# Norm boundaries of a diffusion trunk taken in two token blocks, latents then context

## The reference, cut to what matters

```python
def modulate(x, g, shift, scale):
    return rms_norm(x, g) * (1 + scale) + shift

def macaron_layer(x, mod, norm_g, ffn_in, ffn_out, mixer):
    m = mod[:, :, None, :]
    x = x + 0.5 * m[:, 2] * swiglu(modulate(x, norm_g[0], m[:, 0], m[:, 1]), ffn_in[0], ffn_out[0])
    mixed, own_kv = mixer(modulate(x, norm_g[1], m[:, 3], m[:, 4]))
    x = x + m[:, 5] * mixed
    x = x + 0.5 * m[:, 8] * swiglu(modulate(x, norm_g[2], m[:, 6], m[:, 7]), ffn_in[1], ffn_out[1])
    return x, own_kv
```

## Time and profile before

| | |
|---|---|
| Median of 3 runs | 1470.13 us (1469.03 to 1473.22) |
| The profiled execution | 1469.22 us, its span 1467.4 us |
| TensorE busy | 97% of the span |
| VectorE, ScalarE, GpSimd busy | 66%, 38%, 8% |
| Mean granted TensorE clock | 0.977 of full speed |
| DMA | 243 MB, mean 166 GB/s |

### The profile page before, as it was taken

How to read it: one execution, slowest core, us unless ns; L and a number is a source line. 1 busy time by engine, 2 the same in 40 slices (tenths; PEclk the granted TensorE clock), 3 DMA queues, 4 the chain that set the end, 5 groups by cost and what they waited for, 6 DMA issues and landing times.

```text
span 1467.4 us, 21457 instructions
## 1 busy us (share of the span) xinstructions
PE 1418.3 (97%) x8275; PEld 1388.5 (95%) x8275; DVE 973.9 (66%) x1417; ACT 554.9 (38%) x725; POOL 113.4 (8%) x105
## 2 busy tenths in 40 slices
PE   7999999999858999999999999999999999999999
PEld 5999999999737899999999999999999999999999
DVE  5788879668997668878526788888353459443322
ACT  3433332246575543333224433322345343333320
POOL 0000000016454100000001000000020010000000
PEclk9999999999878999999999999999999999999999
DMA  9765667424100256655341765674333135333432
GB/s 375 280 226 203 236 232 254 162 87 137 52 29 30 101 201 224 234 207 208 115 143 72 262 233 206 220 250 166 137 122 115 62 137 204 125 133 116 142 114 72
DMA packets 46086, 243.02 MB, mean 166 GB/s; under 512 B 5584, under 2 KB 8272, under 8 KB 25424
## 3 DMA queue, kind: packets, MB, share of 16 engines
q1 hardware_dynamic: 45744, 242.16, 45.7%
q10 hardware_dynamic: 288, 0.13, 0.0%
HBM read 240.57 MB, written 1.70 MB: 165 GB/s over the span
## 4 chain that ended last, share of the span: by engine, by line
PE 87%; DVE 9%; ACT 2%; issue 1%; DMA 0%; POOL 0%; SPq 0%; DVEq 0%; ACTq 0%; POOLq 0%
PE ps L1194 28%; PE ps L1196 27%; PE ps L1195 27%; DVE conv L981 4%; PE ps L1283 1%; DVE w_lo L771 1%; PE ps L1257 1%; DVE smax L1046 1%; PE ps L1264 1%; ACT w_hi L516 1%; PE ps L1570 0%; DVE prob L1056 0%; DVE e_sig L1056 0%; DMA x<-in_x_cols 0%; DVE n_full L847 0%
## 5 line engine op out<-in xcount | busy, mean ns | idle before, releaser
L1194 PE MATMUL ps<-a_hi,w_hi 128*128 128x384 f32 x1744 | 587.6, 337 | 4.3 <-DVE a_lo L1061 1.6
L1195 PE MATMUL ps<-a_lo,w_hi 128*128 128x384 f32 x1744 | 583.6, 335 | 0.0
L1196 PE MATMUL ps<-a_hi,w_lo 128*128 128x384 f32 x1744 | 583.5, 335 | 0.0
L771 DVE TENSOR_TENSOR w_lo<-w_raw,w_hi 128x2048 fp32r<-128x2048 f32 x153 | 353.1, 2308 | 213.9 <-ACT w_hi L516 213.9
L516 ACT ACTIVATE w_hi<-w_raw 128x2048 fp32r<-128x2048 f32 x153 | 292.0, 1909 | 239.0 <-DMA w_raw<-in_w_units 239.0
L1194 PEld LDWEIGHTS ps<-a_hi,w_hi 128*128 128x128 f32 x1744 | 328.3, 188 | 12.1 <-issue 3.3
L1195 PEld LDWEIGHTS ps<-a_lo,w_hi 128*128 128x128 f32 x1744 | 328.2, 188 | 0.1
L1196 PEld LDWEIGHTS ps<-a_hi,w_lo 128*128 128x128 f32 x1744 | 328.0, 188 | 0.0
L793 DVE SCALAR_TENSOR_TENSOR m_raw<-m_raw 128x1024 f32<-128x1024 f32 x256 | 299.2, 1220 | 0.0
L1196 PE MATMUL ps<-h_hi,w_lo 128*128 (+1 forms) x704 | 236.6, 336 | 0.0
L1195 PE MATMUL ps<-h_lo,w_hi 128*128 (+1 forms) x704 | 236.5, 336 | 0.0
(11 more groups left out here) (172 smaller groups left out, 710.0 us busy)
## 6 DMA issues: line engine op xcount, KB each, us to landing
w_raw<-in_w_units SPq DMA_DIRECT2D x153, 1024.0 KB, 4.9
m_raw<-in_w_rows SPq DMA_DIRECT2D x128, 512.0 KB, 5.7
m_raw<-in_w_pairs SPq DMA_DIRECT2D x5, 1024.0 KB, 15.6
p_raw<-in_w_pairs SPq DMA_DIRECT2D x3, 1024.0 KB, 24.7
x<-in_x_cols SPq DMA_DIRECT2D x2, 768.0 KB, 5.3
out<-x SPq DMA_DIRECT2D x8, 192.0 KB, 1.9
fourier<-in_k_fourier SPq DMA_DIRECT2D x1, 768.0 KB, 4.5
m_raw<-in_c_ctx SPq DMA_DIRECT2D x1, 512.0 KB, 5.4
```

The costliest lines, as they stand in the source:

```text
L771: nc.vector.tensor_tensor(w_lo[:, slot(u), :], w_raw[:, slot(u), :], w_hi[:, slot(u), :].bitcast(FP32), ALU.subtract).then_inc(lo_done, 1)
L1194: mm(out, whi, mhi, start=start, stop=False)
L1195: mm(out, whi, mlo, start=False, stop=False)
L1196: return mm(out, wlo, mhi, start=False, stop=stop)
```

## The change

The tokens are taken in two blocks, first the 256 latents, then the 128 context tokens (`BLOCKS`). At each of the five boundaries:

- The last two units close together. `closing` runs the 8 output tiles in the order 6, 7, 0 to 5 for the latents (12 matmuls each), then again for the context. The last FFN (s = 5) keeps its old width and only joins its last two units.
- `block_sums` and `block_spread` of the latents stand in TensorE's stream after the third and the fifth context tile of the closing; those of the context stand after the second and the sixth latent tile of the opening. Banks 6 and 7 hold them.
- `first_units` opens two units side by side for the latents, then for the context; at boundary 1 too. Every tile of weights is so loaded twice, once per block.
- Residual, square, scaled, high and low are one operation per tile and block, in an order written out in `turn` (VectorE) and `opening` (ScalarE). GpSimd adds seven squares per block. The splits of the next units stand among them.
- The idle products at boundaries 1 to 5 are gone.
- A load of SP that waits for the second-last unit now waits for both.

```diff
+BLOCKS = [(1, CTX, TOK), (0, 0, CTX)]
+BLOCK_TILES = [range(CTX // P, TT), range(0, CTX // P)]
+D_ORDER = [6, 7, 0, 1, 2, 3, 4, 5]
+ADDED = KT - 1
...
+        def closed(s, blk, i):
+            return 2 * KT * s + KT * blk + i + 1
+        def opened(n, blk, d):
+            return KT + 2 * KT * (n - 1) + KT * blk + d + 1
+        def block_step(n, blk):
+            return 2 * n + blk
...
-                for d in range(1, ADDED):
-                    pool.wait_ge(sq_done, KT * n + d + 1)
-                    if n > 1 or d > 1:
-                        pool.wait_ge(acc_done, (ADDED - 1) * (n - 1) + d - 1)
-                    first = n_sq[:, 0, :] if d == 1 else n_acc[:]
-                    nc.gpsimd.tensor_tensor(n_acc[:], first, n_sq[:, d, :], ALU.add).then_inc(acc_done, 1)
+                for blk, (_, lo, hi) in enumerate(BLOCKS):
+                    for i in range(1, ADDED):
+                        done = (ADDED - 1) * (2 * (n - 1) + blk) + i - 1
+                        pool.wait_ge(sq_done, opened(n, blk, i))
+                        if done:
+                            pool.wait_ge(acc_done, done)
+                        first = n_sq[:, D_ORDER[0], lo:hi] if i == 1 else n_acc[:, lo:hi]
+                        nc.gpsimd.tensor_tensor(n_acc[:, lo:hi], first, n_sq[:, D_ORDER[i], lo:hi], ALU.add).then_inc(acc_done, 1)
...
+            def square(n, blk, i):
+                _, lo, hi = BLOCKS[blk]
+                d = D_ORDER[i]
+                act.wait_ge(x_ready, opened(n, blk, i))
+                nc.scalar.activation(n_sq[:, d, lo:hi], x[:, d, lo:hi], ACT.Square).then_inc(sq_done, 1)
+            def root(n, blk):
+                t = BLOCK_TILES[blk]
+                act.wait_ge(ms_done, block_step(n, blk))
+                nc.scalar.activation(stat[:, 4 + t.start:4 + t.stop], stat[:, t.start:t.stop], ACT.Sqrt).then_inc(root_done, 1)
+            def high(n, blk, d):
+                cnd, lo, hi = BLOCKS[blk]
+                act.wait_ge(full_done, KT + opened(n, blk, d))
+                nc.scalar.activation(a_hi[:, d, lo:hi], n_full[:, d, lo:hi], ACT.Identity,
+                                     bias=m_shift[:, n, d, cnd:cnd + 1]).then_inc(a_hi_done, 1)
+            def opening(n):
+                preload(n, ACT.Sqrt)
+                for i in range(KT):
+                    square(n, 0, i)
+                    if i == 3:
+                        split(UNIT0[n] + 1)
+                square(n, 1, 0)
+                square(n, 1, 1)
+                root(n, 0)
+                square(n, 1, 2)
+                square(n, 1, 3)
+                for d in range(KT):
+                    high(n, 0, d)
+                    if d < 4:
+                        square(n, 1, 4 + d)
+                    if d == 5:
+                        root(n, 1)
+                split(UNIT0[n] + 2)
+                for d in range(KT):
+                    high(n, 1, d)
...
             split(u + 11)
-            split(u + 12)
             act.wait_ge(cache_out, 32)
-            norm_stats(2)
-            norm(2)
+            opening(2)
             ffn(2)
...
+            def residual(s, blk, i):
+                cnd, lo, hi = BLOCKS[blk]
+                d = D_ORDER[i]
+                if blk == 0 or i < KT - 1:
+                    dve.wait_ge(y_done, (2 * KT - 1) * s + KT * blk + i + 1)
+                else:
+                    dve.wait_ge(unit_done, RING + UNIT0[s + 1])
+                nc.vector.scalar_tensor_tensor(x[:, d, lo:hi], ps[:, d, lo:hi], m_gate[:, s, d, cnd:cnd + 1],
+                                               x[:, d, lo:hi], ALU.mult, ALU.add).then_inc(x_ready, 1)
...
+            def mean(n, blk):
+                t = BLOCK_TILES[blk]
+                dve.wait_ge(stat_done, block_step(n, blk))
+                nc.vector.tensor_scalar(stat[:, t.start:t.stop], ps[:, 7, t.start:t.stop], 1.0 / D_MODEL, RMS_EPS,
+                                        ALU.mult, ALU.add).then_inc(ms_done, 1)
+            def diagonal(n, blk):
+                t = BLOCK_TILES[blk]
+                a, b = 8 + t.start, 8 + t.stop
+                dve.wait_ge(root_done, block_step(n, blk))
+                dve.wait_ge(dve_self, mark(nc.vector.reciprocal(stat[:, a:b], stat[:, a - 4:b - 4])))
+                nc.vector.tensor_tensor(n_diag[:, t.start:t.stop, :], ident[:].unsqueeze(1).to_broadcast([P, len(t), P]),
+                                        stat[:, a:b].unsqueeze(2).to_broadcast([P, len(t), P]), ALU.mult).then_inc(diag_done, 1)
...
+            def block_scaled(n, blk, d):
+                cnd, lo, hi = BLOCKS[blk]
+                dve.wait_ge(bc_done, block_step(n, blk))
+                nc.vector.scalar_tensor_tensor(n_full[:, d, lo:hi], ps[:, 6 + blk, lo:hi], m_scale[:, n, d, cnd:cnd + 1],
+                                               x[:, d, lo:hi], ALU.mult, ALU.mult).then_inc(full_done, 1)
+            def block_low(n, blk, d):
+                cnd, lo, hi = BLOCKS[blk]
+                dve.wait_ge(a_hi_done, KT + opened(n, blk, d))
+                nc.vector.scalar_tensor_tensor(a_lo[:, d, lo:hi], n_full[:, d, lo:hi], m_shift[:, n, d, cnd:cnd + 1],
+                                               a_hi[:, d, lo:hi].bitcast(FP32), ALU.add, ALU.subtract).then_inc(a_ready, 1)
+            def turn(s):
+                n = s + 1
+                modulation_gate(s)
+                modulation_in(n)
+                for i in range(KT):
+                    residual(s, 0, i)
+                    if i == 5:
+                        split(UNIT0[n] + 1)
+                residual(s, 1, 0)
+                residual(s, 1, 1)
+                mean(n, 0)
+                diagonal(n, 0)
+                residual(s, 1, 2)
+                residual(s, 1, 3)
+                for d in range(KT):
+                    block_scaled(n, 0, d)
+                    if d < 4:
+                        residual(s, 1, 4 + d)
+                    if d == 6:
+                        mean(n, 1)
+                    if d == 7:
+                        diagonal(n, 1)
+                    if d:
+                        block_low(n, 0, d - 1)
+                block_low(n, 0, KT - 1)
+                for d in range(KT):
+                    block_scaled(n, 1, d)
+                    if d:
+                        block_low(n, 1, d - 1)
+                block_low(n, 1, KT - 1)
...
-            def first_units(u, banks, n, together=True):
+            def first_units(u, banks, n):
+                for blk, (_, lo, hi) in enumerate(BLOCKS):
+                    for m in range(2):
+                        pe.wait_ge(lo_done, RING + u + m + 1)
                     for k in range(KT):
+                        pe.wait_ge(a_ready, opened(n, blk, k))
+                        for m in range(2):
+                            for h in range(2):
+                                ins = three(ps[:, banks[m] + h, lo:hi], tile_of(w_hi, u + m, h * KT + k),
+                                            tile_of(w_lo, u + m, h * KT + k), a_hi[:, k, lo:hi], a_lo[:, k, lo:hi],
+                                            k == 0, k == KT - 1)
+                            if blk == 1 and k == KT - 1:
+                                ins.then_inc(unit_done, 1)
+                        if blk == 0 and k == 1:
+                            block_sums(n, 1)
+                        if blk == 0 and k == 5:
+                            block_spread(n, 1)
...
-            def norm_sums(n):
-
-                for d in range(ADDED, KT):
-                    pe.wait_ge(sq_done, KT * n + d + 1)
-                    token_sums(ps[:, 0, :], n_sq[:, d, :], d - ADDED, False)
-                keep_busy(2)
-                pe.wait_ge(acc_done, (ADDED - 1) * n)
-                token_sums(ps[:, 0, :], n_acc[:], 1, True).then_inc(stat_done, 1)
-
-            def norm_spread(n):
-                pe.wait_ge(diag_done, n + 1)
-                spread(BC_BANK[n], n_diag).then_inc(bc_done, 1)
+            def block_sums(n, blk):
+                t = BLOCK_TILES[blk]
+                pe.wait_ge(x_ready, opened(n, 1, 1))
+                pe.wait_ge(sq_done, opened(n, blk, KT - 1))
+                pe.wait_ge(acc_done, (ADDED - 1) * (2 * (n - 1) + blk + 1))
+                for i, src in enumerate((n_sq[:, D_ORDER[KT - 1], :], n_acc[:])):
+                    for tt in t:
+                        ins = mm(ps[:, 7, tt:tt + 1], src[:, tt * P:(tt + 1) * P], ones[:, 0:1],
+                                 start=(i == 0 and tt == t.start), stop=i == 1, skip_group_check=True)
+                ins.then_inc(stat_done, 1)
+            def block_spread(n, blk):
+                pe.wait_ge(diag_done, block_step(n, blk))
+                for tt in BLOCK_TILES[blk]:
+                    ins = mm(ps[:, 6 + blk, tt * P:(tt + 1) * P], ones[:], n_diag[:, tt, :], start=True, stop=True)
+                ins.then_inc(bc_done, 1)
...
+            def closing(s, pieces):
+                for blk, (_, lo, hi) in enumerate(BLOCKS):
```

(32 more changed lines are left out.)

232 lines of the change are left out of this document (78 added, 154 removed).

## The result

The changed kernel takes 1516.20 us, median of 4 runs (1512.43 to 1521.09), against 1469.73 for the kernel before beside it: ratio 1.0313, 95% interval 1.0277 to 1.035. It is slower by 46.5 us, inside the range of 1474 to 1544, but more than twice the +21.4 that the sum gave. The profiled execution took 1521.09 us, its span 1519.3, the mean granted clock 0.962 where it had been 0.977; it is the slowest of the four runs.

The account below looks back on a forecast made before the run. TensorE's matmul stream and its stops at five boundaries were taken to bound the kernel. Split price 63.5 plus later convolution 6.3 less stall 48.4 gave +21.4 us, forecast 1491.5 us, range 1474 to 1544.

Parts of the forecast that it names:

- the sum: Whole kernel: price 63.5 plus later convolution 6.3 less stall 48.4 gives +21.4 us, 1491.5 us.
- What bounds the kernel: TensorE's matmul stream and its stops at five boundaries; at most 48.4 us to win.
- part 1, the stall goes: At the five boundaries TensorE no longer waits for sums, root, diagonal and scaling; 48.4 us won.
- The covers: TensorE work beside other engines' chains at each boundary: some 1.7 us or more to spare for every added wait.
- Part 2, the price: 192 matmuls per boundary split into 256 and 128 columns (0.118 + 0.111 us), plus sums and spreads: 63.5 us over five boundaries.
- column price: Rival for the split matmuls: 128 columns cost 0.067 us as loads overlap, total 1451 us; chance 0.07.
- plain-f32 price: Rival for the split matmuls: narrow fp32r runs like plain f32, 0.223 us each, total 1599 us; chance 0.10.
- Part 3, the convolution's later start: After boundary 1 both units end together, so VectorE's taps of tile 1 start later: +6.3 us, bounds 4.5 to 6.5.
- The case forecast: All five boundaries at full clock with the stall gone: +21.4 us, 1491.5 us; chance 0.44.
- the first rival: Clock halves after sums in the closing's context block: middle 6, up to 8.3 us per boundary, 1521 us; chance 0.28.

Follow-up runs that it names:

- d_wide_and_sigmoid: Changed kernel with sums 128 columns wide, ScalarE's second sigmoid directly behind the first and VectorE's first taps ahead of a split: 1491.74 us, ratio 1.0159.
- a_wide_sums: Changed kernel with every matmul of the block sums 128 columns wide instead of one: 1493.61 us, ratio 1.0173.
- k_split_earlier: Against a variant with wide sums, half the tiles in blocks and boundary 1's unit 0 opened first: unit 1's split earlier in each closing; 1472.66 us, ratio 1.0028.

## Why the prediction was half right

- **What bounds the kernel; part 1, the stall goes.** Right. At boundary 1 TensorE is busy in every window, with idle time before neither the sums, nor the spread, nor the first opening tile, and the same holds at the others (boundary 2 waits only for the attention's output, as before the change). The covers were enough.
- **Part 2, the price.** Right in mechanism and size. 0.116 to 0.119 us for 256 columns and 0.112 for 128, against 0.118 and 0.111; 46.09 us at boundaries 1, 3 and 4 and 46.41 at 5, against 46.0, once the clock holds. The rivals of a column price (0.067) and of a plain-f32 price (0.223) are out.
- By the Trainium skill (TensorE: Matmul & The Clock Gate, "Back-to-back issue gap") the 128-column pairs would have gone at about 81 ns. The trace shows 112 ns for this fp32r load and matmul, so for this type the measurement decides against it.
- **Part 3, the convolution's later start.** The term was 6.3 us and the attention segment grew by 6.3, with VectorE's taps beginning when forecast, but the mechanism is not shown, and most of the agreement is luck. `d_wide_and_sigmoid` gave the taps their old start back and gained 1.9 us only. What holds the other 4 us is open: TensorE waits 8.0 us for the squares of ScalarE's queries where it waited 3.8, but the kernels that made ScalarE earlier did not win it back.
- **The sum.** The case forecast is the kernel `a_wide_sums`: 1493.61 us against 1491.5. Its span is 25.4 us over before's, not 21.4. The five boundaries make 17.8 of it, where the forecast had 63.5 - 48.4 = 15.1; boundary 2 grew most, by 5.4, since its low stretch of 3.4 us, which used to lie in the gap, now lies among matmuls. The attention segment makes 6.3. The stretch ahead of the first closing makes 1.2; it had 10.2 us at the lower clock and 3.4 before.
- **The rivals: here the step failed.** The forecast priced the new boundaries at a full clock, with nothing for a fall, since "Against it: TensorE never stops" was taken to outweigh the signs for the first rival. That is wrong: TensorE did not stop and the clock fell, which cost 27.1 us. The experiments show what brought it down, the run of single-column sums amid the 128-column matmuls. The rival's own numbers were near: 6 us per boundary, up to 8.3; measured 8.0, 6.4, 6.4 and 6.4 at four boundaries, none at boundary 2. That its 1521 is the profiled 1521.09 is partly luck: that execution is the slowest of four. The median of 1516.2 is lower, and the clocks of the four runs, 0.962 to 0.966, suggest that one stretch fewer fell in two of them. What the profile had to say was in the earlier trace rows and in the 0.67 to 0.82 of the earlier trace rows: the clock was down in those gaps though TensorE was idle for only 0.6 to 1.1 us in each.
- On that, the Trainium skill (TensorE: Matmul & The Clock Gate, "HAM oscillation — how this bites in real kernels") tells of a clock that falls when TensorE waits for data. The fall behind the 1.42 us wait in `k_split_earlier` is of that kind; in the kernel after there was no wait ahead of the four falls, so the advice to avoid idle gaps is not enough here.
- **Chances.** The sign was right. The likelier case, at 0.44, was not the one that came; the rival that did had 0.28.

## What to carry to other kernels

Splitting a matmul of 384 columns in two adds a weight load that the columns no longer hide: the pair took 0.23 us where the whole took 0.173, since no narrow fp32r matmul went under 0.11 us. So split only as many as are needed to cover the chain that follows. Among such half-idle matmuls, make token sums and the like as wide as the load hides anyway (eight records of 128 columns took 0.86 us, eight of one column 0.87) and let TensorE wait for nothing: a run of single-column ones was followed by 10 to 17 us at half the clock in most places, and in one place a wait of 1.4 us was too. A low microsecond cost 0.47 us. When a gap closes, look for the work that another engine did beside it: here the queue behind the first sigmoid, which lost its head start of 8 us. And when a term comes out right to the tenth, test its cause all the same.
